# Conditioning vectors by VectorE, two of six in an opening stage and the others woven into the projections of a fused two-model transformer stack

## The chip, the cores and the metric

One core of one Trainium2 chip runs the whole program as one launch. The metric is the device time in microseconds of that core, the median of several executions. Engines are named as in the profile: PE (TensorE matmuls), PEld (TensorE weight loads), DVE (VectorE), ACT (ScalarE), POOL (GpSimd), SP (SyncE, which only issues transfers here).

## The reference, cut to what matters

256 tokens of width 1024 go through two layers of a first model (an RWKV-7 mixer, then a dilated attention, each followed by a hierarchical mixture of experts), and then two layers of a second model. What the change concerns is the conditioning of the first model: a vector `c` gives six vectors of 1024 per layer.

```python
silu_c = jax.nn.silu(c)
for i in range(DEPTH):                                  # DEPTH = 2
    mod = silu_c @ ada_w[i] + ada_b[i]                  # ada_w[i] is [1024, 6 * 1024], 24 MB
    sh_t, sc_t, ga_t, sh_c, sc_c, ga_c = jnp.split(mod, N_MOD, axis=-1)
    hn = modulate(rms_norm(x, norm_tm_g[i]), sh_t, sc_t)    # h * (1 + scale) + shift
    ...                                                  # mixer (i = 0) or attention (i = 1) of hn
    x = x + ga_t * mixed
    hc = modulate(rms_norm(x, norm_cm_g[i]), sh_c, sc_c)
    x = x + ga_c * hier_moe(hc, ...)
```

The mixer forms six shifted mixes of `hn`, multiplies three of them with `rw_w_rkv` (three 1024 x 1024 matrices) and three with small low-rank matrices (LoRA, `rw_w1`, `rw_a1`, `rw_g1`). The attention multiplies `hn` with `at_w_qkv`, 1024 x 9216. Shifts and scales (spans 0, 1, 3, 4 of the six) are needed as columns, one value for each feature on the partitions; gates (spans 2 and 5) as rows, the same on all partitions.

## The kernel before

All weights stream from HBM in units of 1 MB through `arena`, a ring of 12 slots. `plan_streams` lists the units in the order in which they are used, SP issues their transfers in that order (`ahead`, `issue`), each as soon as its slot is free, and every engine that uses a unit waits until it has landed (`landed`). The counter `k.used` says how many units are done with; a unit's transfer waits until the unit that had its slot is among these. A unit of `ada_w` or of `at_w_qkv` has rows of 4 KB, one of `rw_w_rkv`, `rw_w_o` or the experts 8 KB in a run. The program is a row of phases, each an `nc.Block`. An engine begins the next phase when all engines are through with theirs, SP's issuing in that phase too: a phase's `ahead(k, sp, end)` issues its own units and those behind them that find a slot by then.

The phases that matter, with their helpers:

- `setup_phase`: tokens, positions and `c` are loaded, rotary tables are made; SP issues the first 12 units of `ada_w` and then the ten small loads of `load_router`.
- `ada_phase(k, i)`: 24 units of `ada_w[i]`. For each, PE multiplies the broadcast vector (128 x 32) with it, 512 columns at a time (L478), DVE adds the bias (L510), and PE, DVE and ACT turn the sums into columns (`mod`, `scale_col`) and rows (`gate_row`) (L486 to L522). ACT issues the small loads there, the LoRA matrices of the mixer too (`early`, L452).
- `to_features_phase(norm=...)`: DVE takes the sums of squares (L581), ACT the root (L555), DVE scales the tokens (L590), PE transposes them (L534), and DVE and ACT apply scale and shift (L599, L563).
- `rwkv_project_phase`: DVE makes six mixes `xs` (L799 to L803), two buffers in turn; PE multiplies three of them with four units each (L340, L340, L312), then the LoRAs (L853, L859); POOL builds triangular and block masks at the same time (L741 to L764). DVE normalises the keys (L782 to L784).
- the mixer proper (250 to 545 us), which uses the arena as scratch, so that nothing streams then; `to_features_phase`, and `residual_phase`: four units of `rw_w_o` (PE, L312), and for each of two tiles DVE multiplies with the gate and adds (L630, L631).
- `to_features_phase(norm=1)`, `route_phase`, `experts_phase` (96 units), then `ada_phase(k, 1)`, `to_features_phase(norm=0)`, and `qkv_phase`: nine jobs of four units (L340, L312), two sets of four banks in turn, ACT moving each out (L2172).

Of the kernel before, what the change touches and what calls it, by code (L numbers as in the profile page):

```python
# [23 lines left out]
P = 128  # L24
# [5 lines left out]
SCRATCH = 8  # L30
HALF = 512
# [72 lines left out]
def plan_streams(a):  # L104
# [20 lines left out]
    plan = []  # L125
    for i in range(DEPTH):
        plan.append((f"ada{i}", jobs(a["ada_w"][i], wide(6 * D))))
        if i == 0:
            for j in range(3):
                plan.append((f"rkv{j}", jobs(a["rw_w_rkv"][0, j], wide(D))))  # L130
            plan.append(("stop", 0))
            plan.append(("rwo", jobs(a["rw_w_o"][0], wide(D))))
        else:
            plan.append(("qkv", jobs(a["at_w_qkv"][0], wide(9 * D))))
            plan.append(("taken", SCRATCH))
            plan.append(("awo", jobs(a["at_w_o"][0], wide(D))))
# [19 lines left out]
def make_core(nc, ctx, a):  # L156
# [8 lines left out]
    k.region_w = 21248  # L165
# [9 lines left out]
    k.cond = sb("condition", [P, K8])  # L175
    k.desc = sb("descending", [P, PER_GROUP])
# [17 lines left out]
    k.tile_done = Signal(sem("tile_done"))  # L194
    (k.columns_moved, k.rotated, k.turned_in, k.features_moved, k.index_made, k.index_moved, k.units_scored,
# [34 lines left out]
    for name, units in plan_streams(a):  # L230
# [5 lines left out]
        k.starts[name] = n  # L236
        k.plan += units
# [62 lines left out]
def project_tokens(k, pe, n0, xT, rows, width, set_, per=2, ready=None, tile_done=None, tiles=(0, 1)):  # L300

    halves = [(0, min(HALF, width))] + ([(HALF, width - HALF)] if width > HALF else [])
    for u in range(rows // per):
        landed(k, pe, n0 + u)
        if ready is not None:
            ready(u)
        w = unit(k, n0 + u, width, per)

        def product(kk, tile):
            s = per * u + kk  # L310
            for h, (c0, n) in enumerate(halves):
                mm = pe.matmul(k.ps[:, set_ * 4 + tile * 2 + h, 0:n], xT[:, s, tile * P:(tile + 1) * P],  # L312
                               w[:, kk, c0:c0 + n], start=(s == 0), stop=(s == rows - 1))
            return mm
# [15 lines left out]
def project_features(k, pe, n0, xT, rows, set_, ready=None):  # L330

    for u in range(rows // 2):
        landed(k, pe, n0 + u)
        if ready is not None:
            ready(u)
        w = unit(k, n0 + u, D)
        for kk in range(2):
            s = 2 * u + kk
            for m in range(K8):
                mm = pe.matmul(k.ps[:, set_ * 4 + m // 2, (m % 2) * T:(m % 2 + 1) * T],  # L340
                               w[:, kk, m * P:(m + 1) * P], xT[:, s, :],
                               start=(s == 0 and m % 2 == 0), stop=(s == rows - 1), skip_group_check=True)
        mm.then_inc(k.used, 1)


def setup_phase(k):

    a = k.a
    c = Carver(k.region, k.region_w)
# [4 lines left out]
    places = c.take(PLACES).bitcast(I32)  # L354
    inv = (np.float32(1.0) / np.float32(THETA) ** (np.arange(0, ROT, 2, dtype=np.float32) / np.float32(ROT)))
# [4 lines left out]
    ROUND = float(np.float32(1.5 * 2 ** 23))  # L360

    with k.nc.Block() as block:  # L362
# [19 lines left out]
        def _(vec):  # L382
# [3 lines left out]
            for j in range(ROT // 2):  # L386
                k.vec_chain.mark(vec.memset(freq[:, j:j + 1], float(inv[j])))
# [2584 lines left out]
```

## Time and profile before

| | |
|---|---|
| median of 3 runs | 2831.19 us (2824.17 to 2834.76) |
| the profiled execution's own time | 2822.55 us |
| its span, first to last instruction | 2820.7 us |
| mean granted TensorE clock | 0.937 of full |
| busy PE / DVE / ACT / POOL | 87% / 28% / 14% / 5% of the span |
| read from HBM | 598.41 MB, 213 GB/s over the span |

The busy shares are means over stages with different limits. The opening of the program and the stretch between the first experts and the attention's projections are the stretches to look at one by one; for each, see which engine works, and what the one that works next is waiting for.

### The profile page before, as it was taken

The page shows a single profiled execution, that of the slowest core. Times are in us where ns is not written, and L with a number is a line of the kernel's source. Part 1 is how long each engine was busy: PE and PEld are TensorE (multiplying, and loading weights), DVE is VectorE, ACT ScalarE, POOL GpSimd, SP SyncE. Part 2 cuts the span into 40 slices and gives each one's busy share as a digit, 9 for nine tenths or more (in the row PEclk, how much of TensorE's full clock was granted, in tenths as well). Part 3 has the DMA queues.
Part 4 walks back from the last instruction along what each step waited for, and adds up shares of the span by engine and source line. Part 5 has one row for each costly group of instructions (what it writes and reads, how often), then busy time and mean ns, then how long its engine had stood idle before and what let it go on. Part 6 is the DMA issues. An engine that isn't in the chain of part 4 may idle for free. (4 is left out here: it accounts for less than half of the span.)

```text
span 2820.7 us, 36147 instructions
## 1 busy us (share of the span) xinstructions
PE 2459.5 (87%) x15401; PEld 1327.0 (47%) x15401; DVE 786.4 (28%) x1687; ACT 407.0 (14%) x768; POOL 130.2 (5%) x233
## 2 busy tenths in 40 slices
PE   3397999779997799987999799977999799968997
PEld 0175888643332577774333345434333355433332
DVE  0236576431111200053111253113111351122112
ACT  0002333110000100041000023111000124011001
POOL 0040000001000000000100000000000000001000
PEclk9599999889998899997999899988999899979998
DMA  9610000237999644212799643432999443524995
GB/s 330 255 45 1 3 3 4 105 138 329 421 421 410 267 154 159 90 45 93 299 421 421 245 143 117 179 103 102 420 421 417 152 131 119 187 104 203 421 421 236
DMA packets 137090, 601.85 MB, mean 213 GB/s; under 512 B 32008, under 2 KB 35144, under 8 KB 82144
## 3 DMA queue, kind: packets, MB, share of 16 engines
q1 hardware_dynamic: 126736, 591.65, 53.6%
q10 hardware_dynamic: 10192, 7.86, 0.9%
q8 instruction: 125, 2.05, 0.3%
q14 instruction: 37, 0.30, 0.0%
HBM read 598.41 MB, written 1.05 MB: 213 GB/s over the span
## 5 line engine op out<-in xcount | busy, mean ns | idle before, releaser
L1949 PE MATMUL ps<-arena,region 128*64 128x512 f32 x2048 | 453.6, 595 | 5.3 <-POOL region L2092 5.3
L2489 PE MATMUL ps<-arena,x_features 128*128 128x512 f32 x704 | 323.8, 604 | 3.9 <-PEq L545 3.9
L1949 PEld LDWEIGHTS ps<-arena,region 128*64 128x64 f32 x2048 | 141.4, 137 | 272.1 <-issue 265.2
L1979 PE MATMUL ps<-region 128*128 128x512 f32 x512 | 237.0, 605 | 0.0
L1966 PE MATMUL ps<-arena,region 128*64 128x512 f32 x1024 | 230.8, 592 | 2.1 <-DVE region L2067 2.1
L312 PE MATMUL ps<-arena,region 128*128 128x512 f32 x480 | 213.5, 605 | 14.7 <-PEq L545 11.6
L2074 DVE COPY region<-ps 128x512 f32<-128x512 f32 x64 | 44.4, 693 | 554.5 <-PE ps L1966 554.5
L2489 PEld LDWEIGHTS ps<-arena,x_features 128*128 128x128 f32 x704 | 128.4, 192 | 135.7 <-issue 133.5
L340 PE MATMUL ps<-x_features,arena 128*128 128x256 f32 x768 | 168.0, 382 | 2.5 <-PEq L545 2.5
L1979 PEld LDWEIGHTS ps<-region 128*128 128x128 f32 x512 | 91.7, 189 | 144.2 <-issue 144.2
L2016 ACT ACTIVATE region<-ps 128x512 f32<-128x512 f32 x64 | 38.3, 598 | 833.4 <-PE ps L1966 833.4
L340 PEld LDWEIGHTS ps<-x_features,arena 128*128 128x128 f32 x768 | 147.0, 192 | 24.0 <-issue 3.8
L312 PEld LDWEIGHTS ps<-arena,region 128*128 128x128 f32 x480 | 92.7, 194 | 131.9 <-issue 131.9
L312 PE MATMUL ps<-arena,x_features 128*128 128x512 f32 x320 | 141.9, 605 | 2.6 <-PEq L545 2.6
L1966 PEld LDWEIGHTS ps<-arena,region 128*64 128x64 f32 x1024 | 73.2, 137 | 146.7 <-issue 143.9
L478 PE MATMUL ps<-arena,condition 128*32 128x512 f32 x384 | 64.1, 797 | 73.3 <-PEq L362 42.3
L2092 POOL COPY region<-region 128x512 f32 x128 | 80.8, 634 | 739.4 <-PE ps L1949 688.8
L312 PEld LDWEIGHTS ps<-arena,x_features 128*128 128x128 f32 x320 | 62.0, 195 | 79.9 <-issue 79.7
L2067 DVE COPY region<-ps 128x256 f32<-128x256 f32 x64 | 27.2, 426 | 183.5 <-PE ps L1935 172.3
L1060 PE MATMUL ps<-arena 64*64 64x64 f32 x2304 | 74.5, 219 | 1.4 <-DVE arena L1488 1.2
L1060 PEld LDWEIGHTS ps<-arena 64*64 64x64 f32 x2304 | 69.8, 135 | 6.3 <-issue 4.0
L478 PEld LDWEIGHTS ps<-arena,condition 128*32 128x32 f32 x384 | 12.0, 128 | 122.5 <-issue 65.7
(383 smaller groups left out, 2402.1 us busy)
## 6 DMA issues: line engine op xcount, KB each, us to landing
arena<-in_moe_w_gate SPq DMA_DIRECT2D x64, 1024.0 KB, 11.8
arena<-in_moe_w_up SPq DMA_DIRECT2D x64, 1024.0 KB, 13.9
arena<-in_moe_w_down SPq DMA_DIRECT2D x64, 1024.0 KB, 17.0
arena<-in_w_exp_gate SPq DMA_DIRECT2D x64, 1024.0 KB, 11.1
arena<-in_w_exp_up SPq DMA_DIRECT2D x64, 1024.0 KB, 13.3
arena<-in_w_exp_down SPq DMA_DIRECT2D x64, 1024.0 KB, 16.8
arena<-in_ada_w SPq DMA_DIRECT2D x48, 1024.0 KB, 18.2
arena<-in_w_in SPq DMA_DIRECT2D x40, 1024.0 KB, 5.0
```

Of the source, the lines that this page charges most:

```text
L312: mm = pe.matmul(k.ps[:, set_ * 4 + tile * 2 + h, 0:n], xT[:, s, tile * P:(tile + 1) * P], w[:, kk, c0:c0 + n], start=(s == 0), stop=(s == ...
L340: mm = pe.matmul(k.ps[:, set_ * 4 + m // 2, (m % 2) * T:(m % 2 + 1) * T], w[:, kk, m * P:(m + 1) * P], xT[:, s, :], start=(s == 0 and m % ...
L478: mm = pe.matmul(k.ps[quarter:quarter + 32, j, :], k.cond[:, s:s + 1].to_broadcast([P, 32]), w[:, kk, h * HALF:(h + 1) * HALF], start=(u = ...
L1060: mm = pe.matmul(k.ps[half(cp), bank_, o * CH:(o + 1) * CH], lhsT(half(cp), o), rhs(half(cp), o), start=first and o == 0, stop=True, skip_ ...
L1949: mm = pe.matmul(v3(k.ps[e * CAP:(e + 1) * CAP, 6, :], 2, F), xe[:, q % 2, s, e], w, start=(s == 0), stop=(s == K8 - 1), skip_group_check= ...
L1966: mm = pe.matmul(k.ps[e * CAP:(e + 1) * CAP, 4 + h, :], hidT[:, r, e * CAP:(e + 1) * CAP], w[:, r, h * HALF:(h + 1) * HALF], start=(r == 0 ...
L1979: pe.matmul(k.ps[:, 2 * tile + h, :], gatedT[:, q % 2, tile * P:(tile + 1) * P], out[:, h * HALF:(h + 1) * HALF], start=False, stop=True, ...
L2016: act.activation(out[:, 0:HALF], k.ps[:, 4, :], ACT.Copy).then_inc(k.out_moved0.sem, 1)
L2067: vec.tensor_copy(hidT.rearrange("p r n -> p (r n)"), k.ps[:, 7, 0:T]).then_inc(k.hidden_moved.sem, 1)
L2074: vec.tensor_copy(out[:, HALF:D], k.ps[:, 5, :]).then_inc(k.out_moved1.sem, 1)
L2092: pool.tensor_copy(xe[:, q % 2, :, w], ordered[:, :, bass.ds(first, CAP)]).then_inc(k.window_ready.sem, 1)
L2489: mm = pe.matmul(k.ps[:, 2 * (j % 2) + tile, :], x, row[:, 0:HALF], start=(s_ == 0), stop=(s_ == K8 - 1))
```

## The change

The phases `setup_phase` and `ada_phase` are gone. In their place:

- `condition`: DVE accumulates a unit of `ada_w` into a 128 x 1024 sum, two instructions for each unit: every partition multiplies its own rows of the matrix with its own entries of `c`. The sum over the partitions is left to PE, against a vector of ones: `condition_columns` (eight products of one column) or `condition_rows` (two of 512 columns). The biases are loaded as columns or single rows, and added.
- `opening_phase`: what `setup_phase` did, the norm and the transposes of layer 0, and spans 0 and 1 of layer 0 (8 units). It also makes the mixer's masks, by DVE comparisons of row and column numbers that POOL writes. SP may issue 20 units in it (8 and 12 behind).
- In the projections of the mixer spans 3, 4, 2 and 5 of layer 0 (16 units) lie between the 12 units of `rw_w_rkv`, two behind each of units 1 to 8; in those of the attention the same spans of layer 1, one behind every second unit. PE hands the slot of such a unit back (`release`) with the first matmul of the next one, and waits for `ada_read` ahead of it.
- Spans 0 and 1 of layer 1 (8 units) follow `rw_w_o`. DVE takes six of them before, one between and one behind the two tiles of `residual_phase`; their columns are made in the `to_features_phase` behind it.
- The LoRA matrices are loaded at the start of `rwkv_project_phase` instead, and the router too.

```diff
+EARLY, LATER = (0, 1), (3, 4, 2, 5)
+BESIDE_RKV, BESIDE_QKV = range(1, 9), range(2, 33, 2)
...
+def condition(k, link, vec, n, u, acc):
+    landed(k, vec, n)
+    w = unit(k, n, D)
+    for kk in range(2):
+        s = 2 * u + kk
+        if s == 0:
+            link(vec.tensor_scalar(acc, w[:, kk], k.cond[:, 0:1], None, MUL))
+        else:
+            link(vec.scalar_tensor_tensor(out=acc, in0=w[:, kk], scalar=k.cond[:, s:s + 1], in1=acc, op0=MUL, op1=ADD))
+    vec.sem_inc(k.ada_read.sem, 1)
...
+def condition_columns(k, pe, acc, bank_, m):
+    ones = k.desc[:, PER_GROUP - 1:PER_GROUP]
+    for s in range(K8):
+        mm = pe.matmul(k.ps[:, bank_, m * K8 + s:m * K8 + s + 1], acc[:, s:D:K8], ones, start=True, stop=True)
+    mm.then_inc(k.ada_made.sem, 1)
```

In `opening_phase`, SP, then ACT, then DVE behind masks and norm (`columns` are biases and gains in 32-byte runs, `early` the mixer's vectors):

```diff
+            for tile in range(TILES):
+                sp.dma_start(k.x[:, tile], a["x"][0, tile * P:(tile + 1) * P, :]).then_inc(k.router_landed.sem, 16)
+            ahead(k, sp, n0 + 8)
...
+            act.activation(k.cond[:, :], k.cond[:, :], ACT.Silu).then_inc(k.act_done.sem, 1)
+            for dst, src in (*columns[3:], *b.early):
+                act.dma_start(dst, src).then_inc(k.early_landed.sem, 16)
+
+            act.wait_ge(k.vec_done.sem, k.vec_done.at(1))
+            act.activation(rms, rms, ACT.Sqrt).then_inc(k.act_done.sem, 1)
...
+            for m in range(8):
+                condition(k, link, vec, n0 + m, m % 4, accs[m // 4])
+                if m == 6:
+                    vec.wait_ge(k.early_landed.sem, k.early_landed.at(n_early + 16))
```

In `rwkv_project_phase`, DVE, then PE:

```diff
             for j in range(6):
 
+                if j == 2:
+                    conditions(range(8))
...
+                elif j == 2:
+                    conditions((8, 9))
+                    vec.wait_ge(k.ada_made.sem, k.ada_made.at(2))
+                    condition_out(k, link, vec, 0, 1, 0, 0, LATER[:2])
+                    vec.sem_inc(k.ada_moved.sem, 1)
+                    conditions(range(10, 16))
...
+                m = 4 * j + u
+                if gone(m):
+                    pe.wait_ge(k.ada_read.sem, k.ada_read.at(2 * (m - 1)))
```

In `residual_phase`, SP, then DVE, and the places of the column and row products in `qkv_phase`:

```diff
-            ahead(k, sp, n0 + 4)
+            ahead(k, sp, n0 + 4 + 4 * len(first))
...
+            conditions(range(6))
             for tile in range(TILES):
...
                 link(vec.tensor_tensor(k.x[:, tile], k.x[:, tile], tmp, ADD))
+                conditions((6 + tile,))
...
+    COLUMNS, ROWS = (13, 21), (29, 35)
...
-            phase(f"ada{i}", lambda i=i: ada_phase(k, i, early=rwkv.early if i == 0 else ()))
```

What PE runs from the program's start to the mixer, before. `x4` and the like count the instructions in a row; `region` and `arena` hold inputs and weights, `ps` is the accumulator.

```order
L478 MATMUL ps<-arena,condition 32x512 x96
L486 MATMUL ps<-region 32x512 x8
L491 MATMUL ps<-region 128x512 x4
L497 MATMUL ps<-identity,region 128x128 x8
L534 MATMUL ps<-identity,region 128x128 x16
L837 MATMUL ps<-identity,region 128x64
L340 MATMUL ps<-region,arena 128x256 x128
L312 MATMUL ps<-arena,region 128x512 x24
```

And the same stretch of PE in the change (`descending` holds the ones).

```order
L627 MATMUL ps<-identity,region 128x128 x16
L394 MATMUL ps<-descending,region 128x1 x16
L950 MATMUL ps<-identity,region 128x64
L367 MATMUL ps<-region,arena 128x256 x96
L394 MATMUL ps<-descending,region 128x1 x8
L394 MATMUL ps<-descending,gate_rows 128x1 x8
L367 MATMUL ps<-region,arena 128x256 x32
L337 MATMUL ps<-arena,region 128x512 x24
```

The 96 products with `ada_w` and what made columns and rows of them are gone; 16 one-column products stand ahead of the projections and 16 in the middle of their second job.

DVE in the mixer's projections, in the change, from the second mix on. `L900` are the mixes, eight to a job; before, the first three rows of `L803` there were one row of 24 such instructions with nothing between.

```order
L900 SCALAR_TENSOR_TENSOR region<-region,x_features 128x256 x8
L383 TENSOR_SCALAR region<-arena,condition 128x1024
L385 SCALAR_TENSOR_TENSOR region<-arena,condition,region 128x1024 x7
L383 TENSOR_SCALAR gate_rows<-arena,condition 128x1024
L385 SCALAR_TENSOR_TENSOR gate_rows<-arena,condition,gate_rows 128x1024 x7
L900 SCALAR_TENSOR_TENSOR region<-region,x_features 128x256 x8
```

Sixteen instructions over 1024 columns, eight units' worth, stand now ahead of the third mix.

DVE around the first residual, in the change (`L742`, `L743` are the old L630, L631).

```order
L383 TENSOR_SCALAR region<-arena,condition 128x1024
L385 SCALAR_TENSOR_TENSOR region<-arena,condition,region 128x1024 x3
L742 TENSOR_TENSOR region<-ps,gate_rows 128x1024
L743 TENSOR_TENSOR x_tokens<-x_tokens,region 128x1024
L385 SCALAR_TENSOR_TENSOR region<-arena,condition,region 128x1024 x2
L742 TENSOR_TENSOR region<-ps,gate_rows 128x1024
```

Two of the long instructions have come between the first tile's residual and the second's.

## Rows read from the trace of the kernel before

**Rows 1.** The span in 40 slices of 70.5 us, in tenths, from the page.
```profile
PE   3397999779997799987999799977999799968997
...
DMA  9610000237999644212799643432999443524995
```

**Rows 2.** Stretches: us, busy of PE, PEld, DVE, ACT, POOL, then PEclk, DMA share, GB/s.
```profile
0.00:21.80 21.80, 0.00 (x0) 0.00 (x0) 2.05 (x25) 1.92 (x4) 1.86 (x8) 1.00 0.89 338
...
8.00:36.00 28.00, 0.00 (x0) 0.00 (x0) 1.05 (x6) 0.43 (x2) 0.00 (x0) 1.00 1.03 410
...
42.20:117.90 75.70, 32.84 (x192) 6.21 (x192) 3.91 (x8) 0.00 (x0) 2.66 (x1) 0.62 0.96 362
...
138.80:250.00 111.20, 104.72 (x393) 77.02 (x393) 50.72 (x81) 10.84 (x8) 31.86 (x66) 0.95 0.08 29
...
545.30:554.10 8.80, 3.40 (x16) 3.24 (x16) 1.42 (x4) 1.21 (x4) 0.00 (x0) 0.69 0.89 344
...
640.00:875.00 235.00, 232.18 (x958) 85.37 (x958) 40.37 (x94) 14.10 (x32) 19.92 (x32) 1.00 0.97 402
...
881.50:938.90 57.40, 39.42 (x224) 8.87 (x224) 6.50 (x15) 1.92 (x2) 2.61 (x1) 0.77 1.03 407
...
949.80:1207.00 257.20, 253.64 (x975) 186.36 (x976) 8.69 (x20) 18.92 (x11) 0.45 (x1) 0.99 0.40 135
```

**Rows 3.** Timeline of the opening: start, us, engine, line, operation [idle before].
```profile
2.25 19.54 SPq L261 DMA_DIRECT2D arena<-in_ada_w  x12
...
41.17 0.66 SPq L1637 DMA_DIRECT2D router_bias<-in_moe_router_e_b  x1
...
42.27 14.36 PE L478 MATMUL ps<-arena,condition 128*32 128x512 f32 x112 [42.27 <-PEq L362]
...
127.94 1.23 DVE L581 CUSTOM_DVE_ANT_0 region<-x_tokens 128x1024 f32<-128x1024 f32 x1 [0.57 <-PEq L441]
...
131.06 1.54 DVE L590 TENSOR_SCALAR region<-x_tokens,statistics 128x1024 f32<-128x1024 f32 x2
...
138.85 0.51 DVE L797 COPY region<-x_features 128x2 f32<-128x2 f32 x1 [0.52 <-PEq L545]
```

**Rows 4.** Instructions by line and form: count, busy us, mean ns, idle before.
```profile
L2390 DVE SCALAR_TENSOR_TENSOR x_tokens<-x_tokens,statistics,region 128x1024 f32<-128x1024 f32 x8 | 10.3, 1285 | 0.3
...
L631 DVE TENSOR_TENSOR x_tokens<-x_tokens,region 128x1024 f32<-128x1024 f32 x4 | 4.9, 1225 | 0.1
...
L783 DVE RECIPROCAL arena<-arena 128x1024 f32<-128x1024 f32 x2 | 13.1, 6553 | 0.1
```

**Rows 5.** Timeline rows of small instructions, and of transfers issued by ACT.
```profile
8.03 0.17 DVE L395 TENSOR_SCALAR region<-region 128x16 f32<-128x16 f32 x1
8.24 0.17 DVE L396 SCALAR_TENSOR_TENSOR region<-region 128x16 f32<-128x16 f32 x1
...
64.31 21.23 ACTq L452 DMA_DIRECT2D region<-in_rw_w  x2
...
297.97 1.95 PE L1036 MATMUL ps<-region 128*128 128x2 f32 x16
```

**Rows 6.** Timeline of the mixer's projections.
```profile
141.60 57.46 PE L340 MATMUL ps<-region,arena 128*128 128x256 f32 x256 [2.41 <-DVEq L806]
...
151.31 4.20 DVE L803 SCALAR_TENSOR_TENSOR region<-region,x_features 128x256 f32<-128x256 f32 x8
...
237.70 5.41 PE L853 MATMUL ps<-region 128*128 128x256 f32 x16 [2.04 <-DVEq L806]
```

**Rows 7.** Timeline of the first residual and the router behind it.
```profile
551.43 2.60 SPq L261 DMA_DIRECT2D arena<-in_moe_w_up  x1
...
554.47 29.76 PE L312 MATMUL ps<-arena,region 128*128 128x512 f32 x64 [5.71 <-PEq L545]
...
580.84 1.22 DVE L630 TENSOR_TENSOR region<-ps,gate_rows 128x1024 f32<-128x1024 f32 x1 [30.61 <-PE ps L312]
...
598.30 5.85 PE L1685 MATMUL ps<-router,x_features 128*128 128x36 f32 x32 [2.46 <-PEq L545]
```

More of the change, by code:

```diff
@@ new lines, in condition_columns, with condition_rows @@
+def condition_columns(k, pe, acc, bank_, m):
[3 more added lines that the diff above has]
+    mm.then_inc(k.ada_made.sem, 1)
+def condition_rows(k, pe, acc, bank_):
+    ones = k.desc[:, PER_GROUP - 1:PER_GROUP].to_broadcast([P, P])
+    for h in range(2):
+        mm = pe.matmul(k.ps[:, bank_ + h, :], ones, acc[:, h * HALF:(h + 1) * HALF], start=True, stop=True)
+    mm.then_inc(k.ada_made.sem, 1)
@@ L348, in setup_phase, with add_gate_bias, opening_phase @@
+def add_gate_bias(vec, link, acc, rows, g):
+    for h in range(2):
+        r, c = 32 * (2 * g + h), slice(h * HALF, (h + 1) * HALF)
+        link(vec.tensor_tensor(acc[r:r + 1, c], acc[r:r + 1, c], rows[r:r + 1, :], ADD))
+def opening_phase(k, b):
     a = k.a
-    c = Carver(k.region, k.region_w)
+    n0 = k.starts["first0"]
+    xn = v3(k.region[:, 0:TILES * D], TILES, D)
+    c = Carver(k.region, 3 * TILES * D, TILES * D)
     pos = c.take(TILES).bitcast(I32)
@@ L536, in transposes, with to_features_phase @@
     return mm
-def to_features_phase(k, src, dst, rows, end, norm=None, loaded=0):
+def to_features_phase(k, src, dst, rows, end, norm=None, loaded=0, first=None):
     xn = k.region[:, 0:TILES * D].rearrange("p (t d) -> p t d", t=TILES)
@@ L568, in _ @@
         def _(pe):
+            if first is not None:
+                for m, acc in enumerate(first):
+                    condition_columns(k, pe, acc, 4, m)
             if norm is not None:
@@ L603, in to_features_phase @@
     k.early_landed.close(loaded)
+    if first is not None:
+        k.ada_made.close(2)
     if norm is not None:
@@ L623, in _, with conditions @@
             link = lambda ins: k.vec_chain.link(vec, ins)
+            def conditions(units):
+                for m in units if first else ():
+                    condition(k, link, vec, n0 + 4 + m, m % 4, first[m // 4])
+            conditions(range(6))
             for tile in range(TILES):
@@ L2908, in build @@
         for i in range(DEPTH):
-            phase(f"ada{i}", lambda i=i: ada_phase(k, i, early=rwkv.early if i == 0 else ()))
-            first = "rkv0" if i == 0 else "qkv"
-            phase(f"norm_tm{i}", lambda i=i, f=first: to_features_phase(k, k.x, k.xT, K8, k.starts[f], norm=0))
             if i == 0:
@@ L2933, in moe @@
             def moe(i=i):
-                to_features_phase(k, k.x, k.xT, K8, k.starts[f"moe{i}"], norm=1)
+                to_features_phase(k, k.x, k.xT, K8, k.starts[f"moe{i}"], norm=1, first=k.first if i == 0 else None)
                 route_phase(k, i, k.starts[f"moe{i}"])
```

465 lines of the change are left out of this document (277 added, 188 removed).

## The prediction

> **What bounds the kernel now.** I read the slices of the page first. PE is at 0.9 and more nearly everywhere, but the first two slices hold 3 and 3, while DMA is at 9 and 6; further on the pattern is weaker [rows 1]. So the opening waits for something, and the stretches tell for what. Up to 42.2 us PE does nothing at all: its first matmul waits at a phase boundary, not for weights [rows 3]. SP holds the boundary: its twelve big transfers are issued by 21.8 us, and the ten small router loads behind them only by 41.8 us [rows 3]. From 42.2 to 117.9 us PE is busy for 32.8 us of 75.7, at a DMA share of 0.96: the 24 units of conditions come in no faster than HBM gives them [rows 2]. Then 21 us of small dependent steps make columns, rows and the norm, and the projections' phase starts at 138.8 us [rows 3]. It is PE's: 104.7 of 111.2 us busy, DMA 0.08 [rows 2]. The same conditions for layer 1 take 881.5 to 938.9 us, 57.4 us, DMA at 1.03 [rows 2]. The attention's projections behind them are PE's again (253.6 of 257.2 us) at a DMA share of 0.40 [rows 2]. The reader is to see that the matrices for the conditions are waited for where PE has nothing else, and that next to both stretches lies one of PE work with idle DMA and idle DVE (8.7 us in 257).
>
> **The change, part by part.** First the price of a unit on DVE. Each is two instructions over 1024 columns; of eight, one is a product with a scalar, 0.77 us [rows 3], seven are product and sum of two streams. The latter form took 1.285 us, the two-stream sum 1.225 us [rows 4]; I take 1.22 plus 0.04 between instructions (start to start of small ones 0.21 us at 0.17 each [rows 5]), since the operands are the plain ones of the second row. That is 9.6 us for four units, 2.4 a unit. A unit lands every 2.56 us at 410 GB/s [rows 2]: the two rates are close.
>
> *Opening.* DVE is its chain. Memsets, the numbers from POOL and 22 dependent mask steps at 0.21 us [rows 5] end near 9.6 us, the tokens having landed before. The norm takes from 127.94 to 132.6 us now, 4.7 [rows 3]: 14.4. Seven units, 2 x 0.8 + 12 x 1.26 = 16.7: 31.1, and the seventh has landed at about 24 us. Seven rotary steps 1.5, the eighth unit 2.5: 35.1. Then PE's eight one-column products: 16 records such as L1036, which cost 1.95 us in a busy stretch [rows 5]; the router's 32 records, started behind an idle one, took 5.85 us, 2.9 for 16 [rows 7]. PE has been idle here, so 2.9. Three adds 0.6, four instructions over 256 columns 2.1 (eight took 4.20 us [rows 6]), the rest 0.8: 41.5. SP's issuing is a second candidate for this boundary. When it had issued 12 units (21.8 us), 338 GB/s had brought the tokens and 6.0 units, so about six were outstanding at 4 KB a row [rows 2, 3]; in the first residual, at 8 KB a row, 12 less the 2.9 that 344 GB/s brought, nine [rows 2, 7]. The twentieth unit here goes out when about 13 have landed, near 41 us. I take 42.5 against 138.8: **-96.3 us**.
>
> *Mixer's projections.* PE reaches its third unit about 17 to 19 us into the phase. DVE has then just ended the second mix (151.31 + 4.20 is 16.7 us into it [rows 6], a little sooner without POOL beside it) and needs 4.8 us more to read the two units for which PE waits: +1.4. From there each PE unit takes 57.46 / 8 = 7.2 us [rows 6] against 4.8 of DVE, so the wait doesn't come back. The two sets of columns cost 2 x 1.95 us in the middle of PE's row [rows 5]: +3.9. Units 10 to 15 end DVE at about 65 us into the phase, PE's second job at 65.5, so the fourth mix is not late. The rows (eight records of 29.76 / 64 us [rows 7], 3.7 us of PE) fill the gap up to the fifth mix's products, which wait for DVE as now (2.04 us [rows 6]) and start when they did: 0. PE needs its weights later than they land: 36 units and the tokens, 38.8 MB, are there by 97 us at 410 GB/s [rows 2]. Sum **+5.3**. Queued behind DVE's wait for the LoRA loads (at unit 11) are four units, for which PE's ninth and tenth units wait. ACT issues those loads at the phase's start and I expect them some 56 us into it, where DVE gets there.
>
> *First residual.* This is where the change costs most. SP must issue 4 units of 8 KB rows and 8 of 4 KB before the phase ahead of it may end. By the outstanding counts above they fill 4/9.1 + 8/6.0 = 1.8 of what may be outstanding, so all four and about two more must land first: 6 x 2.56 us behind 546, 561.5, against 554.0 now, when the twelfth unit's issue ended and PE started 0.4 us later [rows 7]: +7.7. DVE's six units (14.4 us) end at 577, ahead of the first tile, which is ready at 588.5. One unit between the tiles and one behind: tile 1 is ready 3.4 us after tile 0 now (554.47 + 29.76 against 580.84 [rows 7]), DVE gets to it 2.5 + 2.5 us after: +1.5, and the last unit +2.5, SP's last issue +0.5. In the norm behind it PE, idle since its projection, makes 16 columns, 5.9 us by the router's row [rows 7], where DVE's sums of squares take 2.9, and DVE has 0.7 us of adds: +3.8. Sum **+16.0**.
>
> *Layer 1.* The phase of 57.4 us goes: **-57.4** [rows 2]. Two sets of columns (3.9) and two of rows go into PE's row, a set of rows being four records of 512 columns at 29.76 / 64 us [rows 7], 1.9: **+7.7**. DVE's 38 us lie beside 257 of PE; 52 units need 133 us of HBM, half of the stretch.
>
> *Experts of layer 0.* Eight more units go ahead of them, 20 us of HBM time; but the slice from 564 to 635 us has DMA at 3 tenths [rows 1], which is room for 49 us, so 0.
>
> Sum -96.3 + 5.3 + 16.0 - 57.4 + 7.7 = -124.7. The profiled execution took 2822.55 us, so 2697.9 by its time; the median of the runs stands 8.6 higher, 2706.5. I say **2702**.
>
> **Rivals.** (A) *ACT is held by its own transfers.* In the opening ACT issues some 3100 runs of 4 to 512 bytes and only then takes the root that DVE's norm waits for. For: two loads of eight rows each held it for 21.23 us while SP was issuing [rows 5]. Against: that was 22 us into its phase, behind the 6144 short runs of the LoRA loads; here they are half as many, in the first microseconds, and the LoRAs come later. By the row DVE resumes up to 20 us late, less 1 us of slack: 2710 to 2722. The Trainium skill (DMA: Bandwidth & Descriptors, Issuing engines are not separate DMA queues) has it that what an issuing engine spends on starting a transfer is usually small beside the transfer; by that rule this rival costs nothing, and the 21.23 us row does not agree with it. (B) *Late LoRA loads.* Their 6144 short runs share the rings with units; if they land 10 us later than I say, PE waits for DVE in its third job: 2709 to 2714. (C) *The boundary before the residual is not held*, because more transfers may be outstanding than I infer: 2694. (D) *The experts of layer 0 run short.* Their DMA share is 0.97 at 402 GB/s [rows 2], and if the first units came late the 20 us would never be made up: 2722. Against: PE is busy for 232.2 of those 235 us [rows 2]. (E) *Slower: DVE's reading becomes the chain.* 32 of the 48 units, 64 instructions, lie on a chain with little slack (opening, mixer, residual). With D us more for each, the loss is about 64 D less 5; it eats 125 us at D = 2.0, an instruction of 3.2 us. At the price of a reciprocal over the same columns, 6.55 us [rows 4], the kernel would take 2702 + 335 = 3040. Against: both rows of the form at 1.2 to 1.3 us. (F) *The change does nothing*, since the stream is the bound anyway: then the projections would have to wait for their weights, and 97 us of streaming lie well inside 42.5 + 116.5.
>
> **How the numbers follow.** Forecast 0.62 (2685 to 2715), A 0.14, B 0.08, C 0.07, D 0.04, E 0.02, F 0.01, 0.02 for what I don't see. The unknown prices bound it: PE's columns 1.95 to 2.9 us a set of eight in five places, SP's hold 0 to 7.7, DVE's form 1.225 to 1.285 (2 us in all). The range 2684 to 2724 takes in A to D. Some 0.5% of the time, 14 us, is what a measurement of this kernel can tell from no change. All cases but E and F are faster: 0.97, 0.01 for no change, 0.02 slower.
>
> **What would show it.** Of the changed profile: projections' phase at 42 to 43 us, with DVE and not a landing as the last wait of the opening; the two-stream form at 1.22 us; one wait of PE of 1 to 4 us ahead of its third unit in the mixer and none at later units; SP's issues in front of the residual ending near 562; PE from the experts' end to the attention's first unit in about 17 us where it is 74 now (875 to 949.8 [rows 2]). Wrong it would be by a root on ACT that comes after 15 us, by matmuls in the mixer's third job that wait for DVE, or by waits for landings in the first experts.

## The result, and the profile of the changed kernel

The changed kernel takes 2724.46 us in the median of 4 runs (2722.72 to 2728.82), the kernel before 2828.15 us in 4 runs beside it (2824.17 to 2834.76). The ratio is 0.9633, with a 95% interval of 0.9609 to 0.9658. It is faster by about 104 us; 2702 us (2684 to 2724) had been predicted. The profiled executions went from a span of 2820.7 to one of 2727.1 us, 93.6 us, and it is this difference that the stages below add up to. (The profiled execution before lay 5.6 us under its kernel's median, the one of the changed kernel 4.4 us over its own, which is why the two differences are 10 us apart. So the miss is 22 us by the medians and 31 us by the stages, where -124.7 had been forecast.)

The slices of the changed kernel's page answer to [rows 1]:

```profile
PE   3989997689998999978998999779997999779996
...
PEclk7989998789998999979999999879999999879998
DMA  9800001839996654035998334425998434426995
```

Before, the first two slices of PE held 3 and 3; now only the first does, and DMA reads 9 and 8 there where it read 9 and 6. The stretches, which answer to [rows 2]; columns are again us, busy of PE, PEld, DVE, ACT, POOL, then PEclk, DMA share, GB/s:

```profile
0.00:51.21 51.21, 11.47 (x48) 11.06 (x49) 36.77 (x97) 6.62 (x11) 3.32 (x15) 0.77 0.98 375
51.21:174.07 122.86, 116.30 (x433) 86.25 (x434) 91.22 (x120) 14.60 (x11) 0.03 (x1) 0.94 0.59 206
...
469.31:486.93 17.62, 3.65 (x17) 3.31 (x17) 1.42 (x4) 1.21 (x4) 0.00 (x0) 0.50 0.95 382
486.93:541.65 54.72, 41.73 (x113) 23.98 (x113) 31.00 (x35) 2.17 (x6) 0.04 (x1) 0.75 0.84 337
541.65:836.33 294.68, 268.82 (x1076) 109.24 (x1076) 67.77 (x178) 25.90 (x48) 21.86 (x38) 0.94 0.84 343
836.33:1103.83 267.50, 265.28 (x1001) 194.76 (x1001) 49.76 (x54) 16.94 (x10) 0.43 (x1) 0.97 0.53 186
```

They are cut at the same instructions in both traces: the start of the mixer's projections, SP's first issue of `rw_w_o`, PE's first matmul of the residual, the router, the attention's first projection, and the first of the scores behind it. The table puts the forecast beside them; each difference is the length of a stage after less that before.

| stage | before, us | after, us | difference | forecast |
|---|---|---|---|---|
| opening, to the mixer's projections | 138.85 | 51.21 | -87.6 | -96.3 |
| projections and mixer, to SP's issue of `rw_w_o` | 406.46 | 418.10 | +11.6 | +5.3 |
| that issue to the residual's first matmul | 9.16 | 17.62 | +8.5 | +7.7 |
| residual and norm, to the router | 43.83 | 54.72 | +10.9 | +8.3 |
| experts of layer 0, to the attention's projections | 351.53 | 294.68 | -56.9 | -57.4 |
| attention's projections | 252.30 | 267.50 | +15.2 | +7.7 |
| all behind them | 1618.57 | 1623.27 | +4.7 | 0 |
| sum | | | -93.6 | -124.7 |

Two stages came out as forecast within a microsecond. Four did not: the opening, the mixer's projections and the attention's by 6 to 9 us each, residual and norm by 2.6. Nothing had been forecast for the last row, and nothing was changed there.

The opening of the changed kernel, in the timeline that answers to [rows 3]. The number in brackets is the idle time before, and what ended it:

```profile
7.76 7.22 ACTq L594 DMA_DIRECT2D region<-in_rw_w  x1
...
11.96 1.22 DVE L545 CUSTOM_DVE_ANT_0 region<-x_tokens 128x1024 f32<-128x1024 f32 x1
...
14.37 0.17 DVE L548 TENSOR_SCALAR statistics<-statistics 128x2 f32<-128x2 f32 x1
...
17.66 1.28 ACT L597 ACT_TABLE_LOAD   x1 [13.25 <-issue]
18.96 0.20 ACT L597 ACTIVATE statistics<-statistics 128x2 f32<-128x2 f32 x1
...
19.19 0.17 DVE L552 RECIPROCAL statistics<-statistics 128x2 f32<-128x2 f32 x1 [4.65 <-ACT statistics L597]
...
43.67 3.94 PE L394 MATMUL ps<-descending,region 128*128 128x1 f32 x16 [8.12 <-DVEq L386]
...
47.65 0.37 DVE L412 TENSOR_TENSOR mod_columns<-ps,condition_columns 128x8 f32<-128x8 f32 x2 [4.17 <-PE ps L394]
```

DVE has its sums of squares at 14.54 us and then waits 4.65 us for a root. ACT was not computing in that time: it stood in the issuing of its row loads, one of which held it for 7.22 us, and loaded the table for the root only at 17.66 us. At the end DVE waits 4.17 us for PE's second set of columns. No landing ends the opening.

The mixer's projections, in PE's timeline, answer to [rows 6]:

```profile
71.39 27.86 PE L367 MATMUL ps<-region,arena 128*128 128x256 f32 x128 [1.08 <-DVEq L386]
99.09 3.75 PE L394 MATMUL ps<-descending,region 128*128 128x1 f32 x16
102.71 3.94 PE L394 MATMUL ps<-descending,gate_rows 128*128 128x1 f32 x16
106.51 15.72 PE L367 MATMUL ps<-region,arena 128*128 128x256 f32 x64
```

The wait ahead of the third unit is there, 1.08 us, and it does not come back. The two sets of columns cost 3.75 and 3.94 us of PE, not 1.95 each. And the 64 matmuls behind them took 15.72 us where the 128 ahead took 27.86, 13.93 for 64: from 106.5 to 110 us PE's granted clock was 0.51 of full.

### The profile page after: what moved, and what is told of

Same layout as the page of the kernel before. It is cut to its first block and busy times, and to the rows that moved or that the text cites. A ratio compares the mean times of both kernels' runs of the same rounds, so it can differ in the third digit from the quotient of the medians.

```text
span 2727.1 us, 35676 instructions
## 1 busy us (share of the span) xinstructions
PE 2429.7 (89%) x15097; PEld 1350.6 (50%) x15097; DVE 906.7 (33%) x1816; ACT 407.7 (15%) x769; POOL 94.4 (3%) x172
## 5 line engine op out<-in xcount | busy, mean ns | idle before, releaser
L627 PE MATMUL ps<-identity,region 128*128 128x128 f32 x120 | 25.4, 395 | 53.5 <-DVEq L555 21.1
L385 DVE SCALAR_TENSOR_TENSOR gate_rows<-arena,condition,gate_rows 128x1024 f32<-128x1024 f32 x49 | 62.9, 1284 | 17.1 <-DMA arena<-in_ada_w 13.3
## 6 DMA issues: line engine op xcount, KB each, us to landing
arena<-in_moe_w_up SPq DMA_DIRECT2D x64, 1024.0 KB, 13.7
```

The source lines that it names most:

```text
L385: link(vec.scalar_tensor_tensor(out=acc, in0=w[:, kk], scalar=k.cond[:, s:s + 1], in1=acc, op0=MUL, op1=ADD))
```

## The experiments

The changed kernel once more, and eleven kernels made from it. Times are medians of 4 or 5 runs, and ratios are to the kernel before, which ran beside each group of four (2825.80, 2826.32 and 2826.57 us). Where a kernel is said to be so much under or over the changed kernel, it is against the 2724.39 us of the first of these runs.

**The changed kernel once more.**

> The changed kernel as it stands, as the measure for the three kernels beside it. The theory: nothing but scatter parts it from the first profile, 2724 us within 3, and the stages repeat to 0.5 us: projections' phase at 51.2 us, residual's first matmul at 486.9, router at 541.7, attention's projections from 836.3 to 1103.8. The rival: the 4.7 us that the changed kernel's execution lost behind the attention's projections are scatter, so that this stretch (1623.3 us to the end) comes out nearer to the 1618.6 of the kernel before.

2724.39 us, ratio 0.9649 (0.9636 to 0.9662). Most stages repeat to about a microsecond: projections at 51.15 us, residual at 487.45, router at 540.95. Two lengths do not. The attention's projections took 264.80 us, not 267.50. The windows just behind PE's second set of columns there show why (us, PE's busy time, PEclk, DMA share, GB/s); first the changed kernel's first trace, then this one:

```profile
991.00:994.00 3.00, 3.00 (x8) 0.50 0.58 238
994.00:998.00 4.00, 4.00 (x6) 0.58 0.73 246
```

```profile
990.30:994.00 3.70, 3.70 (x10) 1.00 0.63 188
994.00:1010.00 16.00, 16.00 (x38) 1.00 0.59 214
```

In the one the clock fell behind the set, in the other it did not, with the same instructions ahead. And the part behind them took 1622.60 us, so the rival, which had it back at 1618.6, was not borne out here; but over all fourteen traces of this study, in which this part of the program is the same, it took 1616.28 to 1625.24 us, the kernel before 1618.57. The 4.7 us of the last row lie inside what equal instructions scatter by, and so a difference of two spans is good to no better than some 5 us either way. What scatters is PE's busy time for the same 5437 matmuls: 1452.0 us in the shortest of these fourteen parts, 1455.1 in the kernel before, 1459.2 in the changed one and 1461.3 in the longest. Read in stretches of 20 us, the granted clock stood at half for an estimated 180 us of the shortest and 210 us of the longest.

**ACT's root ahead of its row loads.**

```diff
-            for dst, src in (*columns[3:], *b.early):
-                act.dma_start(dst, src).then_inc(k.early_landed.sem, 16)
-
             act.wait_ge(k.vec_done.sem, k.vec_done.at(1))
             act.activation(rms, rms, ACT.Sqrt).then_inc(k.act_done.sem, 1)
+            for dst, src in (*columns[3:], *b.early):
+                act.dma_start(dst, src).then_inc(k.early_landed.sem, 16)
```

> In the opening ACT takes the root of the norm before it issues its rows of biases and the mixer's vectors; nothing else differs. Theory (ACT is held by its own transfers): the wait of 4.65 us in front of DVE's reciprocal shrinks to about 0.5 (the root itself and its table load may still follow the statistics), the projections' phase starts near 47 us instead of 51.2, and the kernel is 4 us faster. Rival: what DVE waits for is the table load of the root (it came 17.66 us into the program, just ahead of the root at 18.96), which stays behind the statistics: gain 3 us or less. Second rival: the loads, issued later, land after DVE's seventh unit and the wait comes back there: 0 us.

2729.03 us, ratio 0.9667 (0.9654 to 0.9680): not faster, and since this interval overlaps that of the changed kernel, the totals alone don't show it slower either. The timeline of this kernel shows both halves of it:

```profile
14.87 0.17 DVE L552 RECIPROCAL statistics<-statistics 128x2 f32<-128x2 f32 x1 [0.33 <-ACT statistics L595]
...
26.34 0.58 ACTq L597 DMA_DIRECT2D region<-in_rw_k_a  x1
...
44.04 0.17 DVE L561 CAST region<-region 128x2 f32<-128x2 int32 x1 [9.22 <-DMA region<-in_rw_k_a]
```

The root came 4.3 us earlier, at the cost that the first theory gave it. But the last small load, issued at 26.34 us, landed only at 44.0, and DVE, which asks for all of them at its seventh unit, stood there for 9.22 us. The second rival had named the place; the price, a projections' phase at 55.96 us, 4.8 later than in the changed kernel instead of even with it, is beyond what it said.

**The same, with DVE asking at its seventh unit for the positions alone** (and for the other loads only ahead of the adds that use them).

> In the opening alone: ACT takes the root before it issues the row loads, and DVE waits at its seventh unit for the positions alone, and for the other small loads only ahead of its adds. Theory (ACT held by its own transfers cost 4.65 us, and the loads' landing at 44 us stands just behind PE's second set of columns): the projections' phase at 47.6 us instead of 51.2, and the kernel 3.6 us faster, 2720.8. Rival: what the projections' phase gains is lost in it, because the conditions' units are not there earlier (DVE waits for landings at its next eight units): 1 us or less.

2722.25 us, ratio 0.9636 (0.9623 to 0.9649). The projections' phase started at 47.54 us, 3.6 earlier, as the theory said; the whole kernel's gain of 2.1 us is within what the two intervals leave open.

**The boundary in front of the first residual, not held.**

```diff
-            ahead(k, sp, end)
+            if upto is not None:
+                issue(k, sp, upto)
+            else:
+                ahead(k, sp, end)
...
-                    to_features_phase(k, og, k.mixT, K8, k.starts["rwo"])
+                    to_features_phase(k, og, k.mixT, K8, k.starts["rwo"], upto=k.starts["rwo"] + 4)
```

> The stage in front of the first residual issues only the four units of the output matrix, and the eight units of conditions are issued in the residual's own phase; nothing else differs. Theory (SP's issuing, held by how many transfers are outstanding, holds the boundary): PE starts its residual projection near 478.5 us instead of 486.9, and the kernel is 7 to 8 us faster, since DVE, which gets its units at the same time, has 25 us until the first tile. Rival: the four units of 8 KB rows land late as well, PE starts only when the first has landed, and DVE's six units then reach past the first tile: gain 4 us or less.

2712.70 us, ratio 0.9603 (0.9589 to 0.9616), 11.7 us under the changed kernel. SP's and PE's timelines:

```profile
468.98 1.93 SPq L286 DMA_DIRECT2D arena<-in_rw_w_o  x4
...
474.80 12.28 SPq L286 DMA_DIRECT2D arena<-in_ada_w  x8
...
474.86 29.60 PE L337 MATMUL ps<-arena,region 128*128 128x512 f32 x64 [1.99 <-PEq L638]
```

PE starts 5.9 us behind SP's first issue, where the changed kernel takes 17.6 and the kernel before 9.2. So it is SP's issuing in that phase that held the boundary, as the prediction had it (that SP in its turn is held by the number of outstanding transfers was argued from counts and is not tested by this), and the gain exceeds the 7 to 8 us because part of the hold was there before the change.

**PE's load of neighbouring columns, the stride moved to DVE.** DVE reads its unit as 8 columns of 128 with a step of 8 and writes blocks.

```diff
+    if turned:
+        w = w.rearrange("p a (q k) -> p a k q", k=K8)
+        acc = acc.rearrange("p (k q) -> p k q", k=K8)
...
-        mm = pe.matmul(k.ps[:, bank_, m * K8 + s:m * K8 + s + 1], acc[:, s:D:K8], ones, start=True, stop=True)
+        mm = pe.matmul(k.ps[:, bank_, m * K8 + s:m * K8 + s + 1], acc[:, s * P:(s + 1) * P], ones, start=True, stop=True)
```

> The sums for shifts and scales are kept with the stride on DVE's side: DVE reads its unit in steps of 8 columns and writes 8 blocks of 128, and PE loads 128 neighbouring columns in each one-column product, instead of every eighth of 1024. Theory A (PE's strided load is what makes a set 3.75 us and a weight load 335 ns): a set costs 1.9 to 2.2 us, and eight sets save some 13 us, if DVE's form keeps its 1.28 us. Theory B (the price is that of a product of one column behind its own weight load, whatever the stride): a set stays at 3.7 us and the kernel at the time of the one it was made from. Theory C: DVE's strided reading costs more than PE saves; at D us more for each of 64 instructions on the chain it loses up to 64 D, slower than the changed kernel from D = 0.2 on.

2737.21 us, ratio 0.9689 (0.9676 to 0.9702), 12.8 us over the changed kernel: theory C. DVE's two-stream form over 1024 columns went from a mean of 1284 ns to 2067, D = 0.78. But theory A holds too, in the attention, where DVE has slack; the first fence holds the products' weight loads and matmuls in the changed kernel run again (ns, minimum/median/maximum, then the first and the last start), the second those of this kernel:

```profile
L394 PEld LDWEIGHTS ps<-descending,gate_rows x48: 312/335/336, 102.6 to 990.0; 128*128 128x128 f32 x48
L394 PE MATMUL ps<-descending,gate_rows x48: 167/376/377, 102.6 to 990.0; 128*128 128x1 f32 x48
```

```profile
L397 PEld LDWEIGHTS ps<-descending,gate_rows x48: 190/192/333, 121.9 to 1010.5; 128*128 128x128 f32 x48
```

and its timeline in the attention:

```profile
951.90 1.84 PE L397 MATMUL ps<-descending,gate_rows 128*128 128x1 f32 x16
953.60 48.59 PE L367 MATMUL ps<-x_features,arena 128*128 128x256 f32 x224
```

A set there costs 1.84 us instead of 3.75, and the attention's projections 259.31 us instead of 264.80 to 267.50. Of these 5.5 to 8.2 us the two sets themselves are 3.8; the rest is the clock, which stayed at 1.00 behind both sets here.

**Only PE's load changed.** The shifts and scales come out in another order of the features, and this kernel leaves out what would put them right.

> The eight one-column products of a set load 128 neighbouring columns of the sum instead of every eighth of 1024; DVE's reading is as in the changed kernel. Shifts and scales so come in another order of the features, and the work is the same otherwise. Theory (the strided load is the price): where PE's clock is full, a set falls from 3.75 to 1.84 us, as it did in the attention with DVE's reading turned, and the matmuls behind the first of the attention's sets, 224 in 50.28 us, take 48.6; where the clock is at half (opening, residual's norm) only from 3.94 to 3.55. Mixer's projections 4 to 6 us shorter, attention's 5.4, the rest 1: 10 to 12 us faster than the changed kernel, 2713. Rival (it was DVE, reading the sum's neighbours in strides, that freed PE's port, or the products find the clock down anyway): sets stay above 3 us and the time within 4 us of the changed kernel.

2716.29 us, ratio 0.9607 (0.9593 to 0.9621), 8.1 us under the changed kernel. The weight loads of the sets in the middle of busy stretches, PE's timeline of the mixer's sets, and the windows over them:

```profile
L394 PEld LDWEIGHTS ps<-descending,gate_rows x48: 190/192/192, 100.4 to 980.2; 128*128 128x128 f32 x48
...
98.70 1.84 PE L394 MATMUL ps<-descending,region 128*128 128x1 f32 x16
100.40 1.93 PE L394 MATMUL ps<-descending,gate_rows 128*128 128x1 f32 x16
102.19 14.06 PE L367 MATMUL ps<-region,arena 128*128 128x256 f32 x64
```

```profile
100.40:102.20 1.80, 1.80 (x19) 1.00 1.03 410
102.20:106.00 3.80, 3.80 (x20) 1.00 1.04 420
```

The mixer's second job ends 65.28 us into the phase (70.86 and 71.72 in the two traces of the changed kernel); the prediction's sum for this point had been 65.5. The attention's projections take 259.31 us, 7.0 more than before, where 7.7 had been forecast. DVE reads as in the changed kernel here and with a step in the kernel above, and both give 259.31, so it is PE's load and nothing on DVE's side that matters there. By mixer and attention this kernel gains 11.7 to 13.7 us on the two traces of the changed kernel; against the second of them its execution lost 1.6 us in the experts and 2.4 behind the attention, where the instructions are the same.

**Both in their right order, at two instructions' worth of DVE time.** In the attention as two kernels above; in the mixer the last accumulating instruction of each span writes in blocks.

```diff
+            out = acc if last is None or s < K8 - 1 else last.rearrange("p (k q) -> p q k", k=K8)
...
+    turned = [b.v[:, m] for m in range(2)]
```

> The changed kernel with PE's loads of neighbouring columns in the mixer and the attention, and shifts and scales in their right order: in the attention DVE reads its units in steps of 8 columns, in the mixer the last accumulating instruction of each of the two spans writes in blocks. Theory (the price was the strided load, and DVE can turn the sums for two instructions' worth of time): mixer 6 us and attention 5.5 us shorter, 2715, within 2 us of the kernel that only changed the load. Rival: the strided write costs like a strided read for the whole matrix and PE waits for it at its third unit: 2718 or more.

2714.87 us, ratio 0.9604 (0.9591 to 0.9617): as forecast. The two turned writes took 2.01 and 2.03 us against 1.28. Its mixer's second job ends 66.97 us into the phase, 1.7 later than in the kernel that only changed the load, and that is the clock: behind the same sets, at 1.00 throughout here,

```profile
98.30:100.30 2.00, 2.00 (x20) 1.00 0.99 401
100.30:102.00 1.70, 1.70 (x17) 1.00 1.03 412
102.00:106.00 4.00, 4.00 (x14) 0.64 1.04 423
```

it fell to 0.64, where it had stayed at 1.00 in the kernel above. So of the 6 us that the kernel above gained in the mixer, 3.9 are the sets and come with the load; the other 2 hang on the clock, which did not always stay up.

**A third instruction for every unit.**

```diff
+    link(vec.scalar_tensor_tensor(out=acc, in0=acc, scalar=1.0, in1=acc, op0=MUL, op1=MAX))
     vec.sem_inc(k.ada_read.sem, 1)
```

> A third two-stream instruction for each of the 48 units (the maximum of the sum with itself, which leaves it as it is): DVE's price of a unit goes from 2.6 to 3.9 us. It sizes the slack that the prediction gave the chain. By the prediction's formula for a slower reading (64 D less 5, D = 0.64 us for each of two instructions) it costs 36 us. Rival: the chain is only the opening's eight units and the one unit behind the residual's second tile, and elsewhere DVE has slack: 12 to 15 us.

2755.16 us, ratio 0.9742 (0.9725 to 0.9759), 30.8 us more than the changed kernel. The opening grows by 10.1 us, the mixer by 13, the residual with its norm by 2 to 3, the attention by nothing that its scatter would show. The formula's 36 us was near, and in part by luck. It had the residual's six units on the chain, which they are not: PE's 26 us up to the first tile cover even units of 3.9 us. And the stages with the units account for some 26 us of the 31; the rest lies in stages whose lengths scatter by as much.

**Layer 1 as before.**

> Layer 0 as changed, layer 1 as before: 24 units in a phase of their own behind the first experts, plain projections in the attention, nothing but the output matrix in the first residual. If the stages add up as the two traces read, the changed kernel's layer 1 is worth -56.9 (the phase) + 15.2 (attention's projections) + 8.5 + 10.9 (first residual and its norm), -22.3 us in all, and this kernel comes at 2747, 78 us under the kernel before. Rival: layer 0's eight units in the first residual cost less than read there, because the kernel before had the same hold of SP: then this kernel lies further from the changed one, 2755 or more. By the prediction's sums (layer 1 at -57.4 + 7.7 + 16.0 = -33.7) it would be 2758.

2745.19 us, ratio 0.9716 (0.9700 to 0.9733), against 2747 expected. So the changed kernel's layer 1 is worth 20.8 us, layer 0 with the opening 81. The residual's first matmul comes 8.9 us behind SP's first issue here; with only units of 8 KB rows to issue, the hold is that of the kernel before.

**Columns of span 0 made at the residual's end.**

> The changed kernel, but the columns of span 0 for layer 1 are made at the end of the first residual's projection and not in the norm behind it. Theory: the products there lie on the chain because PE does two sets, 7.74 us, while DVE has 2.9 us of sums of squares; one set of 3.9 leaves a wait of 1.3 us where there are 5.15: 3.8 us faster, 2720.6. Rival: DVE waits for the root of ACT there anyway and the gain is 2 us or less.

2723.86 us, ratio 0.9636 (0.9623 to 0.9649). DVE's wait in the norm falls from 5.16 to 1.35 us, and the way from residual to router from 53.5 to 51.3 us. That a whole kernel is 3 us faster these medians do not show.

**Three edits, and five.**

> Three edits to the changed kernel together: the first residual's boundary is not held (worth 11.7 us alone); in the opening ACT takes the root first and DVE waits at its seventh unit for the positions alone, for the rest only where it uses them (4.3 to 4.6 us, if the loads, which landed at 44.0 us when issued behind the root, come ahead of PE's second set of columns at about 43 to 47 us); in the attention alone the columns' sums are kept with the stride on DVE's side, which has slack there (5.4 us). Theory: they add up, 21 us under the changed kernel, 2703. Rival: the late small loads hold DVE once more, now ahead of its adds, and the opening gives nothing: 2707.

2705.86 us, ratio 0.9569 (0.9555 to 0.9582), 18.5 us under the changed kernel, between theory and rival: the projections' phase starts at 47.60 us, with 0.7 us of DVE's 4.84 us wait due to a small load that landed at 44.0.

> The three edits of the kernel at 2705.9 us, and two more: in the mixer the last of the eight accumulating instructions of spans 3 and 4 writes its result in 8 blocks of 128, so that PE's loads are of neighbouring columns there too; and in the first residual PE makes the columns of span 0 behind its projection, where it waits for DVE anyway, so that the norm behind it has one set to make instead of two. Theory: the mixer's second job ends at 65.3 us into the phase instead of 71 to 71.8 (as with the plain load), 6 us, and the norm's wait of DVE for PE's sets (5.15 us) falls to 1.3, 3.9 us: 2696. Rival: the strided writes of DVE, 0.8 us each, come back as PE's wait at its third unit, and PE's clock, down by then, makes the early set no cheaper: 2701.

2698.98 us, ratio 0.9548 (0.9535 to 0.9561), the fastest of the study, 25.4 us under the changed kernel. From residual to router it takes 50.8 us instead of 54.1 in the kernel with three edits. The mixer's second job ends at 68.6 us, not 65.3. The turned writes are not the cause: PE waits 1.95 us ahead of its third unit, but it starts that unit 20.2 us into the phase, as in the changed kernel and in the two kernels above with neighbouring loads (where the first two units run faster, the wait is longer by as much). All 3.3 us arise from the sets on, where the clock fell although the loads are of neighbours. Timeline and windows:

```profile
95.53 4.79 PE L400 MATMUL ps<-descending,region 128*128 128x1 f32 x32
```

```profile
97.00:101.00 4.00, 4.00 (x22) 0.59 1.05 423
101.00:105.00 4.00, 4.00 (x11) 0.55 0.93 349
```

## Why the prediction was off, step by step

Its direction and its mechanism held: the conditions' phases are gone, layer 1's is worth -56.9 us against -57.4, PE goes from the experts' end to the attention's first unit in 16.4 us (17 had been said), and PE waits for no landing in the mixer's projections, the first experts and the attention's projections. The hold of SP in front of the residual was there with +8.5 for +7.7, and taking it away gave 11.7 us. What was off were sizes, all on the same side.

**The price of a column set was the step that failed.** The prediction took it from "16 records such as L1036", 1.95 us in a busy stretch, 2.9 behind an idle PE. That row loads 128 neighbouring columns; the new products load every eighth of 1024. The weight loads of that row, in the kernel before:

```profile
L1036 PEld LDWEIGHTS ps<-region x64: 186/192/192, 298.0 to 498.6; 128*128 128x128 f32 x64
```

Those of the new products took 335 ns, and a set 3.75 us at full clock and 3.94 at half. The kernel that changed only the load put the set back to 1.84 us, and with it the mixer to the forecast point (65.28 for 65.5) and the attention to +7.0 for +7.7. In the attention the account closes: the strided load costs 5.5 to 8.2 us there, 3.8 for the two sets and the rest for the clock behind them. Behind the strided sets of the attention the clock fell to half for 3 to 6 us in 11 places of 14 (seven traces), behind sets with neighbouring loads in none of 10 (five traces), and the stage's length follows: 259.31 us without a fall, 264.8 with one, 267.5 to 267.6 with two. In the mixer the sets are 3.9 us (7.69 for 3.77). That the match at 65.28 is so close is partly luck with the clock: with neighbouring loads it fell there in three kernels of four, and the same point came at 66.97 and 68.6 in two of them.

Where PE had been idle the price failed too, but less by the stride. In the norm the sets took 7.74 us where 5.9 had been put, which is 1.8 of the 2.6 us missing there; with neighbouring loads they still took 6.96, and one set in the opening 3.54 instead of 3.94. The router's row was the wrong one for them: its 5.85 us ran at a granted clock of 0.61 of full, the norm's sets at 0.50.

The Trainium skill (Advanced Engine Details and Errata, SBUF Cachelines) states that reads which touch a line of 16 bytes only once pay a penalty, and that the stride that does no harm depends on the type. A step of 32 bytes touches another line each time, and two measurements agree with it: 335 to 192 ns for PE's load at full clock, 2067 to 1284 ns for DVE's form. At half the clock PE's load shows nothing of it, 335 to 333 ns. It had not been weighed in the prediction.

**The opening's 8.7 us are four small things.** ACT's root: +4.4 against a norm of 4.7 us, which is rival A at a quarter of its bound. The mask steps ended at 11.96 us and not at 9.6, +2.4: the 22 of them began at 5.70 us, where the forecast's sum has them begin near 5.0, and took 6.26 us instead of 4.6, since ten with two operations came 0.32 us apart and ten sums 0.26, against the 0.21 assumed from rows of 16 columns (these have 64). The reading: 21.09 to 39.29 us for seven units, 18.2 instead of 16.7, and 0.4 on the eighth. The column set: +1.0, of which the stride is 0.4. The sum, 9.7, is 1 more than the miss, because the forecast had rounded its own 41.5 up to 42.5. That ACT's root would come in time was a wait put at nothing. Of rival A the prediction had said the right thing about the row of 21.23 us [rows 5] and still given it 0.14: one of the loads of eight rows, 4 KB, held ACT for 7.22 us here, while SP was issuing big ones. (That SP's transfers are the cause is argued; that ACT's own issuing stood before the root is shown by moving it.) The Trainium skill's rule (DMA: Bandwidth & Descriptors, Issuing engines are not separate DMA queues), that starting a transfer is usually small beside it, does not agree with these 7.22 us for 4 KB either.

**The two-stream form** took 1.284 us, the upper bound and not the 1.22 chosen: with a scalar operand it goes by the row of the same operation [rows 4], not by that of the plain sum.

**The other marks.** One wait ahead of PE's third unit, 1.08 us in the profiled execution, 0.42 to 1.95 in the others in which DVE reads its first units in the same way: right, though in five of them shorter than the 1 us that had been the least. No wait for the LoRA loads: rival B did not occur. No landing waits in the experts: D did not. C (2694, boundary not held) is what the kernel without the hold makes of it, at 2712.7. E's formula, 64 D less 5, gave 36 us for a measured 31, near by luck in part, as said above.

**What stays open.** When PE's clock falls behind sets with neighbouring loads. In the attention, where a set stands alone, it never did (ten places). In the mixer, where two follow each other, it fell in three kernels (0.50 to 0.64 behind the sets; in one of them PE had also waited 1.8 us just ahead) and stayed at 1.00 in a fourth, with the same products. And why the granted clock behind the attention stood at half for longer in one execution than in another is not known.

## What to carry to other kernels

Price a new instruction from a row with the same access pattern, not only the same shape: a step of eight words cost PE's weight load 1.7 times its time at full clock, and DVE's form 1.6 times, and where both engines could carry the stride, one turned write (0.7 us more) did what eight strided loads or eight strided reads had done. When an engine issues transfers and also stands on a chain, put the compute ahead of the issuing, then look at who waits for the landings, since a small load issued behind big ones may land 18 us later: moving one without the other started the next phase 4.8 us later. And a phase boundary should carry only the issues that the next phase needs at its start; here that alone was worth 11.7 us.

## What the runs showed of the hardware

- A one-column product whose weights are every eighth 4-byte word: weight load 335 ns (192 with neighbours), eight of them in two passes 3.75 us (1.84). At half the granted clock the weight load took 333 ns with neighbours and 335 strided, the set 3.55 and 3.94 us, so that the stride costs much only where the clock is full. (In the openings of seven traces the profile reads 1.00 for the granted clock from the start, with sets of 3.54 and 3.93 us. That reading does not fit what PE did: in the changed kernel run again five matmuls of 256 columns came in the 2 us from 54 and eleven in the 2 us from 60, both at 1.00.)
- DVE, 1024 columns, product with a scalar and sum: 1284 ns plain, 2067 with the matrix read in steps of 8 words and the sum kept in blocks, 2007 to 2025 with only the write in steps, of 128 words.
- Behind strided sets amid busy stretches the granted clock fell to half in 11 places of 14 in the attention and, where two sets follow each other in the mixer, in 8 of 8; with neighbouring loads in none of 10 and in 3 of 4.
- One transfer of eight rows issued by ACT beside SP's 1 MB ones held it for 7.22 us; in another kernel a small one issued at 26.3 us landed at 44.0.
- Equal instructions behind the attention took between 1616.28 and 1625.24 us over fourteen traces.
